# A macaron transformer block on one core: abs ahead of relu in the stick-breaking scores, and ten steps of the mixer in another place

## The chip, the cores and the metric

The kernel runs on one core of one Trainium2 chip. The metric is the device time of one execution in microseconds (us). The engines are named as in the profile: PE is TensorE (matmuls), DVE is VectorE, ACT is ScalarE, POOL is GpSimd, and SP issues the DMAs. Each engine works through its own list of instructions in order; they meet only at semaphores.

## What is computed

One block of three sublayers over 512 tokens of width 1024, in float32, each with RMSNorm and a modulation (`ada`) from a conditioning vector: a SwiGLU FFN of width 2816, a token mixer, and a second such FFN. The mixer, cut to what matters here:

```python
def stick_breaking_attention(q, k, v):          # 8 heads of 64
    z = einsum('bqhd,bkhd->bhqk', q, k) * scale
    log_beta = log_sigmoid(z)
    log_keep = where(strict, log_beta - z, 0.0)
    suffix = cumsum(log_keep, axis=3, reverse=True) - log_keep
    w = where(strict, exp(log_beta + suffix), 0.0)
    return einsum('bhqk,bkhd->bqhd', w, v)

def forgetting_attention(q, k, v, log_f_cum):   # 8 heads of 64, q and k normed
    z = einsum('bqhd,bkhd->bhqk', q, k) * scale + log_f_cum(q) - log_f_cum(k)
    return einsum('bhqk,bkhd->bqhd', softmax(where(causal, z, -inf)), v)

proj = h @ w_in                                  # q, k, v of both kinds, gates, forget logits
mix = concatenate([rmsnorm(o_sb), rmsnorm(o_fx) * sigmoid(fox_gate)]) @ w_out
x = x + gate * mix
```

## The kernel before

**Stages.** The first FFN runs to about 400 us of the trace, the mixer from there to about 730 us, the second FFN after it. Weights are not used as they are: each tile of 128x1024 is split into a rounded high part (`w_hi`, ACT, L1107) and the rest (`w_lo`, DVE, L1471), and each product is three matmuls (L694 to L696). Four raw tiles and two split ones are kept at a time; the load of tile t by SP waits until tile t-4 is split.

**Jobs and units.** The mixer has eight jobs of two heads each: jobs 0 to 3 are stick-breaking, 4 to 7 forgetting. A job has five units, each a 128x512 block of scores made up of the causal blocks of one or two query blocks. `(j, u)` below is unit u of job j. The scores of successive units go to bank 2 and bank 3 in turn.

**The order** is one list, `STEPS`, which `mixer_steps` writes out and which PE, ACT, DVE all walk; each engine issues what the step asks of it and skips the rest. So moving a step moves its instructions on every engine that it uses. The kinds of step are:

- `proj` (PE: half a weight tile against h; q, k and gate chunks use bank 0 or 1, v chunks both), `out` (PE: the output projection)
- `split` (ACT then DVE: the next weight tile)
- `evac` (ACT then DVE: a finished chunk is copied out of its bank into q, k or v as high and low part; for a gate chunk DVE first copies it, L1781, then ACT makes the sigmoid in three passes, L1303 to L1307)
- `scores` (PE, L960 to L962), `prep`, `sum`, `exp` (the pointwise work, below), `turn` (PE: transpose, L984), `unload` (ACT L1402 then DVE L1889: the transposed block as `pt_hi` and `pt_lo`)
- `values` (PE: weights times v into bank 6; half 0 needs units 0 to 2 of its job unloaded, half 1 all five)
- `square`, `stat`, `scale`, `part` (the RMSNorm of a head pair: ACT squares, L1331; PE takes the mean, L1012; ACT makes 1/rms, L1338 and L1340, DVE multiplies, L1804; ACT and DVE write high and low part, for o L1349 and L1816, for q L1356 and L1823)
- `forget`, `decay` (the forget gates' running sum, and its rows on PE, L1021, and ACT, L1366).

**A stick-breaking unit** goes through a chain: scores on PE; in `prep` DVE takes relu of the bank (L1839, `relu_done`), then ACT takes abs of the same bank (L1374), exp (L1376) and ln (L1378); in `sum` DVE scans (L1867) and subtracts (L1871); in `exp` ACT takes exp (L1394); PE turns, ACT and DVE unload. ACT's abs waits for `relu_done`:

```python
act.wait_ge(relu_done, unit + 1)        # ACT, L1371
if unit >= 2:
    act.wait_ge(scan_done, unit - 1)
a(buf, bank[2 + unit % 2][:], ACT.Abs).then_inc(abs_done, 1)
```

Within one unit's period DVE's list reads: relu, scan, subtract, the low part of an `evac`, the low part of a `split`, the low part of the unload of the unit before, and then the relu of the next unit. ACT's reads: abs, exp, ln, high parts of `evac`, `split` and unload, the unit's last exp, and then the abs of the next unit.

Of the kernel before, what the change touches and what calls it, by code (L numbers as in the profile page):

```python
# [22 lines left out]
SBJ = 4  # L23
# [67 lines left out]
def halves_due(p):  # L91

    return int(6 + 1.65 * min(p + 1, 5) + 1.55 * min(max(p - 4, 0), 20) + 0.95 * max(p - 24, 0))


def mixer_steps():
# [13 lines left out]
    steps, norms, chains, evacs, splits = [], [], [], [], []  # L110
# [3 lines left out]
    def emit(*step):  # L114
        steps.append(step)
        spent[0] += array.get(step[0], 0)
# [154 lines left out]
    for n in range(4):  # L271
        emit("out", n, KC - 1, KC)
    assert not queue
    return steps, norms


STEPS, NORMS = mixer_steps()


def hybrid_block_kernel(  # L280
# [4 lines left out]
    with ctx:  # L285
        def sem(name):
            return ctx.enter_context(nc.semaphore(name))
# [14 lines left out]
        def keep(name, shape, dt=F32):  # L302
# [127 lines left out]
        s_done, relu_done, abs_done, eneg_done, e_ready, scan_done, d_ready, p_ready_sb = (  # L430
            sem("s_done"), sem("relu_done"), sem("abs_done"), sem("eneg_done"), sem("e_ready"),
            sem("scan_done"), sem("d_ready"), sem("p_ready_sb"))
# [656 lines left out]
        def _(act):  # L1089
# [176 lines left out]
            for step in STEPS:  # L1266
# [93 lines left out]
                elif kind == "decay":  # L1360
                    _, j, h = step
# [5 lines left out]
                elif kind == "prep" and step[1] < SBJ:  # L1367

                    unit = 5 * step[1] + step[2]
                    buf = tmp_a[:, unit % 2, :]  # L1370
                    act.wait_ge(relu_done, unit + 1)  # L1371
                    if unit >= 2:
                        act.wait_ge(scan_done, unit - 1)
                    a(buf, bank[2 + unit % 2][:], ACT.Abs).then_inc(abs_done, 1)  # L1374
# [4 lines left out]
                elif kind == "prep":  # L1379

                    _, j, u = step
                    unit = 5 * j + u
# [8 lines left out]
                elif kind == "exp" and step[1] < SBJ:  # L1391
                    unit = 5 * step[1] + step[2]
                    act.wait_ge(d_ready, unit + 1)
                    a(tmp_b[:, unit % 2, :], tmp_b[:, unit % 2, :], ACT.Exp).then_inc(p_ready_sb, 1)  # L1394
                elif kind == "unload":
                    _, j, u = step
                    unit = 5 * j + u
# [53 lines left out]
            for tb in range(TB):  # L1451
# [5 lines left out]
                  scale=1.0 / D).then_inc(fln_done, 1)  # L1457
# [5 lines left out]
        def _(dve):  # L1463
# [201 lines left out]
            with dve.Fori(0, UP_BLOCKS) as i:  # L1665
                for q in range(4):
                    f, j = 4 * i + 2 + q, q % 2
# [61 lines left out]
            for step in STEPS:  # L1729
# [101 lines left out]
                elif kind == "prep":  # L1831
                    _, j, u = step
                    unit = 5 * j + u
                    zb, buf = bank[2 + unit % 2], tmp_b[:, unit % 2, :]
                    dve.wait_ge(s_done, unit + 1)
                    if unit >= 2:
                        dve.wait_ge(t_done, unit - 1)
                    if j < SBJ:
# [18 lines left out]
                elif kind == "sum" and step[1] < SBJ:  # L1857

                    _, j, u = step
                    unit = 5 * j + u  # L1860
# [11 lines left out]
                elif kind == "sum":  # L1872
                    _, j, u = step
                    unit = 5 * j + u
# [9 lines left out]
                elif kind == "unload":  # L1884
                    _, j, u = step
                    unit = 5 * j + u
# [79 lines left out]
```

## Time and profile before

| what | us |
|---|---|
| median of 3 runs | 1145.46 |
| lowest, highest | 1144.56, 1147.65 |
| profiled execution, its time | 1145.88 |
| its span in the trace | 1144.1 |

The profiled execution lies 0.42 us above the median, and 1.8 us of it are outside the span. PE is busy for 1108.5 us of the span. The granted clock is TensorE's: 1.00 is 2.4 GHz, 0.50 is 1.2 GHz. In the rows of the trace a matmul's end is modelled and overlaps the start of the next, so that an idle time of PE is some 0.2 us shorter in a row than the time by which the next matmul is late; the prediction says where it adds that.

### The profile page before, as it was taken

How to read it: one execution, taken by the hardware profiler on the slowest of the kernel's cores; microseconds unless marked ns; L12 is line 12 of the kernel's file. 1: busy time of each engine (PE TensorE's matmuls, PEld its weight loads, DVE VectorE, ACT ScalarE, POOL GpSimd, SP SyncE). 2: the span in 40 equal slices, each digit the busy share in tenths (PEclk: the TensorE clock that was granted, in tenths of full speed). 3: DMA queues.
4: the chain of work that ended last, by engine and by line, in shares of the span. 5: the costliest groups of instructions: out<-in, count | busy, mean ns of one | idle time of the engine just before them, and what ended most of it. 6: DMA issues, size and time to landing. Idle time of an engine off the chain costs nothing.

```text
span 1144.1 us, 14298 instructions
## 1 busy us (share of the span) xinstructions
PE 1108.5 (97%) x5142; PEld 885.2 (77%) x5142; DVE 596.1 (52%) x829; ACT 446.4 (39%) x693; POOL 71.7 (6%) x68
## 2 busy tenths in 40 slices
PE   8999999999999999889999999999999999999997
PEld 5788888888788868678778767778888888878876
DVE  3746464655644556777766677663333333434343
ACT  5522222222222235566776665353222222312312
POOL 1000000000000001000000000000000000225350
PEclk9999999999999999999999999999999999999999
DMA  9755675565573631221212211332333333223221
GB/s 343 212 148 165 195 207 166 165 190 165 166 227 105 193 92 47 80 67 44 73 52 66 65 47 42 89 91 74 92 97 96 97 94 92 74 83 98 96 92 74
DMA packets 169687, 133.32 MB, mean 117 GB/s; under 512 B 5436, under 2 KB 150956, under 8 KB 169644
## 3 DMA queue, kind: packets, MB, share of 16 engines
q1 hardware_dynamic: 168704, 130.60, 38.0%
q0 software_dynamic: 768, 2.10, 0.8%
q8 instruction: 26, 0.43, 0.2%
q14 instruction: 17, 0.14, 0.0%
q10 hardware_dynamic: 172, 0.06, 0.0%
HBM read 128.54 MB, written 2.10 MB: 114 GB/s over the span
## 4 chain that ended last, share of the span: by engine, by line
PE 76%; DVE 12%; ACT 7%; issue 3%; DMA 1%; SPq 0%; DVEq 0%; ACTq 0%
PE bank L694 24%; PE bank L696 24%; PE bank L695 24%; DVE w_lo L1471 2%; DVE tmp_b L1867 2%; DVE pt_lo L1889 1%; PE bank L714 1%; ACT w_hi L1107 1%; ACT tmp_a L1376 1%; DVE tmp_b L1839 1%; ACT tmp_a L1374 1%; ACT tmp_a L1378 1%; DMA w_raw<-in_w_ffn_down_dram 1%; PE bank L1012 1%; DVE tmp_b L1871 1%
## 5 line engine op out<-in xcount | busy, mean ns | idle before, releaser
L1471 DVE TENSOR_TENSOR w_lo<-w_raw,w_hi 128x1024 fp32r<-128x1024 f32 x163 | 216.9, 1332 | 382.6 <-ACT w_hi L1107 382.1
L694 PE MATMUL bank<-h_hi,w_hi 128*128 128x512 f32 x864 | 349.2, 404 | 1.3 <-DVE v_lo L1772 0.3
L695 PE MATMUL bank<-h_lo,w_hi 128*128 128x512 f32 x864 | 342.9, 397 | 0.0
L696 PE MATMUL bank<-h_hi,w_lo 128*128 128x512 f32 x864 | 342.8, 397 | 0.0
L1107 ACT ACTIVATE w_hi<-w_raw 128x1024 fp32r<-128x1024 f32 x163 | 172.3, 1058 | 422.2 <-PE bank L696 402.5
L694 PEld LDWEIGHTS bank<-h_hi,w_hi 128*128 128x128 f32 x864 | 163.2, 189 | 44.9 <-issue 5.5
L695 PEld LDWEIGHTS bank<-h_lo,w_hi 128*128 128x128 f32 x864 | 163.1, 189 | 40.6 <-issue 2.6
L696 PEld LDWEIGHTS bank<-h_hi,w_lo 128*128 128x128 f32 x864 | 163.1, 189 | 39.6
L595 POOL TENSOR_TENSOR w_raw<-w_raw,gate_row 128x1024 f32<-128x1024 f32 (+1 forms) x24 | 54.9, 2287 | 378.9 <-DMA w_raw<-in_w_ffn_down_dram 378.6
L694 PE MATMUL bank<-w_hi,hid_hi 128*128 128x512 f32 x176 | 69.9, 397 | 3.2 <-DVE w_lo L1471 3.2
L694 PE MATMUL bank<-hid_hi,w_hi 128*128 128x512 f32 x176 | 70.1, 398 | 1.0 <-DVE w_lo L1471 1.0
L696 PE MATMUL bank<-w_hi,hid_lo 128*128 128x512 f32 x176 | 69.8, 396 | 0.0
L696 PE MATMUL bank<-hid_hi,w_lo 128*128 128x512 f32 x176 | 69.8, 396 | 0.0
L695 PE MATMUL bank<-hid_lo,w_hi 128*128 128x512 f32 x176 | 69.8, 396 | 0.0
L695 PE MATMUL bank<-w_lo,hid_hi 128*128 128x512 f32 x176 | 69.2, 393 | 0.0
L1483 DVE SCALAR_TENSOR_TENSOR ada_acc<-ada_w,cond,ada_acc 128x1024 f32<-128x1024 f32 x49 | 62.7, 1279 | 0.0
L1216 ACT ACTIVATE hid_hi<-tmp_b 128x512 f32 (+1 forms) x44 | 27.8, 632 | 85.6 <-DVE tmp_b L1663 81.1
L1598 DVE TENSOR_TENSOR hid_lo<-tmp_b,hid_hi 128x512 f32 (+1 forms) x44 | 30.5, 692 | 39.7 <-ACT hid_hi L1216 39.6
L1867 DVE TENSOR_TENSOR_SCAN tmp_b<-tmp_a,tmp_b 128x512 f32<-128x512 f32 (+3 forms) x32 | 25.1, 815 | 36.0 <-ACT tmp_a L1378 36.0
L694 PEld LDWEIGHTS bank<-w_hi,hid_hi 128*128 128x128 f32 x176 | 33.0, 188 | 11.7 <-DVE w_lo L1471 4.0
L694 PEld LDWEIGHTS bank<-hid_hi,w_hi 128*128 128x128 f32 x176 | 33.1, 188 | 9.3 <-DVE w_lo L1471 1.4
L696 PEld LDWEIGHTS bank<-hid_hi,w_lo 128*128 128x128 f32 x176 | 33.1, 188 | 8.1
(215 smaller groups left out, 1342.6 us busy)
## 6 DMA issues: line engine op xcount, KB each, us to landing
w_raw<-in_w_ffn_up_dram SPq DMA_DIRECT2D x88, 512.0 KB, 4.6
ada_w<-in_w_ada_dram SPq DMA_DIRECT2D x56, 512.0 KB, 3.6
w_raw<-in_w_ffn_down_dram SPq DMA_DIRECT2D x36, 512.0 KB, 4.4
w_raw<-in_w_in_dram SPq DMA_DIRECT2D x28, 512.0 KB, 3.7
ada_first<-in_w_ada_dram SPq DMA_DIRECT2D x16, 512.0 KB, 10.9
w_raw<-in_w_out_dram SPq DMA_DIRECT2D x8, 512.0 KB, 3.7
w_raw<-in_w_ffn_down_dram SPq DMA_DIRECT2D x8, 384.0 KB, 4.4
x_nat<-in_x_dram SPq DMA_DIRECT2D x4, 512.0 KB, 5.2
```

The lines of the kernel that those rows point to most:

```text
L595: g.tensor_tensor(tile, tile, gate_row[:, :, half * 512:(half + 1) * 512] .broadcast_to([P, nk, 512]), ALU.mult).then_inc(w_gated, 1)
L694: mm(dst, wh, xh, start=start, stop=False, skip_group_check=skip)
L695: mm(dst, wh, xl, start=False, stop=False, skip_group_check=skip)
L696: return mm(dst, wl, xh, start=False, stop=stop, skip_group_check=skip)
L714: last = mm(bank[4 + p][:], cond[:, k:k + 1].broadcast_to([P, P]), ada_first[:, p, k, :], start=k == 0, stop=k == KC - 1)
L1012: mm(bank[7][:], pair_mean[:], ssum[:], start=True, stop=True).then_inc(stat_done, 1)
L1107: a(w_hi[:, s, :], w_raw[:, r, :], ACT.Copy).then_inc(w_hi_done, 1)
L1216: a(hid_hi[:, bass.ds(f, 1), :], tmp_b[:, j:j + 1, :], ACT.Copy).then_inc(hid_hi_done, 1)
L1471: v.tensor_tensor(w_lo[:, s, :], w_raw[:, r, :], w_hi[:, s, :].bitcast(F32), ALU.subtract)\
L1483: ins = v.scalar_tensor_tensor(ada_acc[:], source, cond[:, k:k + 1], ada_acc[:], ALU.mult, ALU.add)
L1598: v.tensor_tensor(hid_lo[:, bass.ds(f, 1), :], tmp_b[:, j:j + 1, :], hid_hi[:, bass.ds(f, 1), :].bitcast(F32), ALU.subtract).then_inc(hid_ ...
L1867: last = v.tensor_tensor_scan(buf[:, back], tmp_a[:, unit % 2, back], buf[:, back], 0.0, ALU.add, ALU.add)
```

## The change

**The order of abs and relu.** In the stick-breaking units ACT's abs now waits for the scores themselves, and DVE's relu waits for ACT's abs. No instruction is added or removed. The forgetting units keep their wait.

**The moved steps.** After the list is written, ten steps are taken out and put in front of another step, in this order:

```diff
+AHEAD = (
+    (("prep", 0, 1), ("forget", 4)),
+    (("evac", 15), ("scores", 4, 1)),
+    (("split", 83), ("exp", 2, 3)),
+    (("split", 93), ("part", 10)),
+    (("split", 95), ("part", 13)),
+    (("part", 11), ("scores", 6, 1)),
+    (("scores", 2, 0), ("proj", 78, 8, 0)),
+    (("scores", 2, 3), ("stat", 1)),
+    (("proj", 88, 17, 0), ("stat", 7)),
+    (("prep", 6, 1), ("scale", 11)),
+)
...
+    for step, mark in AHEAD:
+        steps.remove(step)
+        steps.insert(steps.index(mark), step)
     return steps, norms
...
-                    act.wait_ge(relu_done, unit + 1)
+                    act.wait_ge(s_done, unit + 1)
                     if unit >= 2:
                         act.wait_ge(scan_done, unit - 1)
                     a(buf, bank[2 + unit % 2][:], ACT.Abs).then_inc(abs_done, 1)
...
-                    dve.wait_ge(s_done, unit + 1)
+                    if j < SBJ:
+                        dve.wait_ge(abs_done, unit + 1)
+                    else:
+                        dve.wait_ge(s_done, unit + 1)
```

Five of the ten go to a later place, though the table is called AHEAD: the gate copy `evac 15`, the splits 83, 93 and 95, and `part 11`. The other five go earlier: two `prep`, two `scores`, and one half of `proj 88`. In the changed kernel the lines after the table are numbered 17 higher, those of DVE's loop behind the new wait 20 higher.

DVE around unit (2, 3), before: `split 83` (the row of `w_lo_52`) stands ahead of the unload of (2, 2) (the two rows of `pt_lo_96`), and relu waits for the scores (`s_done`).

```order
L1792 TENSOR_TENSOR k_l_b_94<-bank1,k_hh_b_93 64x512
L1471 TENSOR_TENSOR w_lo_52<-w_raw_50,w_hi_51 128x1024 [waits w_hi_done]
L1889 TENSOR_TENSOR pt_lo_96<-bank4,pt_hi_95 128x2x128 [waits pt_hi_done]
L1889 TENSOR_TENSOR pt_lo_96<-bank4,pt_hi_95 128x2x128
L1839 TENSOR_SCALAR tmp_b_70<-bank2 128x512 [waits t_done,s_done]
```

The same place now:

```order
L1809 TENSOR_TENSOR k_l_b_94<-bank1,k_hh_b_93 64x512
L1909 TENSOR_TENSOR pt_lo_96<-bank4,pt_hi_95 128x2x128 [waits pt_hi_done]
L1909 TENSOR_TENSOR pt_lo_96<-bank4,pt_hi_95 128x2x128
L1488 TENSOR_TENSOR w_lo_52<-w_raw_50,w_hi_51 128x1024 [waits w_hi_done]
L1859 TENSOR_SCALAR tmp_b_70<-bank2 128x512 [waits t_done,abs_done]
```

The unload has passed the split, and relu waits for `abs_done`.

PE ahead of the first v tile of chunk 8, before: the scores of unit (1, 4) into bank 3, then `proj 78`, whose first matmul waits until the chunk before it is out of bank 0 and 1 (`v_ready`).

```order
L960 MATMUL bank3<-k_hh_b_93,q_st_92 128x512 [waits d_ready]
L961 MATMUL bank3<-k_l_b_94,q_st_92 128x512
L962 MATMUL bank3<-mask_strict_55,ident_bf_54 128x128
L694 MATMUL bank0<-w_hi_51,h_hi_74 128x256 [waits v_ready,w_lo_done]
L695 MATMUL bank0<-w_lo_52,h_hi_74 128x256
```

Now:

```order
L977 MATMUL bank3<-k_hh_b_93,q_st_92 128x512 [waits d_ready]
L978 MATMUL bank3<-k_l_b_94,q_st_92 128x512
L979 MATMUL bank3<-mask_strict_55,ident_bf_54 128x128
L977 MATMUL bank2<-k_hh_a_99,q_st_92 128x512 [waits d_ready,qk_ready,k_twice0]
L978 MATMUL bank2<-k_l_a_100,q_st_92 128x512
L979 MATMUL bank2<-mask_strict_55,ident_bf_54 128x128
L711 MATMUL bank0<-w_hi_51,h_hi_74 128x256 [waits v_ready,w_lo_done]
```

The scores of unit (2, 0) have come between the two; the scores of (2, 3) go ahead of `stat 1` and `proj 80` in the same manner.

DVE around job 6's first units, before: `scale 11` (`nrm_104`), `sum` of (6, 0), `part 11` (the low part of q for job 7), the unload of (5, 4), and then `prep` of (6, 1) from bank 3.

```order
L1804 TENSOR_TENSOR nrm_104<-bank0,rstd_73 128x512 [waits nrm_lo,nrstd_done]
L1878 RECIPROCAL small_68<-small_68 128x1 [waits exp_done,nrm_f32]
L1882 TENSOR_SCALAR tmp_b_70<-tmp_b_70,small_68 128x512 [waits inv_done]
L1823 SCALAR_TENSOR_TENSOR q_st_92<-nrm_104,gq8_66,q_st_92 64x512 [waits nrm_hi]
L1823 SCALAR_TENSOR_TENSOR q_st_92<-nrm_104,gq8_66,q_st_92 64x512
L1889 TENSOR_TENSOR pt_lo_96<-bank5,pt_hi_95 128x4x128 [waits pt_hi_done]
L1849 ISA tmp_b_70,small_68<-bank3,f_keys_101 128x384 [waits exp_done,t_done,s_done]
```

Now:

```order
L1869 ISA tmp_b_70,small_68<-bank3,f_keys_101 128x384 [waits exp_done,t_done,s_done]
L1869 ISA small_68 128x1
L1869 ISA tmp_b_70,small_68<-bank3,f_keys_101 128x128
L1869 ISA small_68 128x1
L1875 TENSOR_SCALAR small_68<-small_68 128x2 [waits max_done]
L1821 TENSOR_TENSOR nrm_104<-bank0,rstd_73 128x512 [waits nrm_lo,nrstd_done]
L1898 RECIPROCAL small_68<-small_68 128x1 [waits exp_done,nrm_f32]
L1902 TENSOR_SCALAR tmp_b_70<-tmp_b_70,small_68 128x512 [waits inv_done]
L1909 TENSOR_TENSOR pt_lo_96<-bank5,pt_hi_95 128x4x128 [waits pt_hi_done]
L1840 SCALAR_TENSOR_TENSOR q_st_92<-nrm_104,gq8_66,q_st_92 64x512 [waits nrm_hi]
L1840 SCALAR_TENSOR_TENSOR q_st_92<-nrm_104,gq8_66,q_st_92 64x512
```

`prep` of (6, 1) now leads, and the unload has passed `part 11`.

## Rows read from the trace of the kernel before

**Rows 1.** Busy time, share of the span and instructions of each engine, from the page.

```profile
PE 1108.5 (97%) x5142; PEld 885.2 (77%) x5142; DVE 596.1 (52%) x829; ACT 446.4 (39%) x693; POOL 71.7 (6%) x68
```

**Rows 2.** Windows: stretch, its length, busy us of PE, PEld, DVE, ACT, POOL; clock.

```profile
442.00:600.00 158.00, 143.93 (x804) 118.40 (x803) 111.28 (x165) 108.95 (x187) 5.13 (x11) 0.98 0.24 64
600.00:730.00 130.00, 124.49 (x662) 100.28 (x662) 87.25 (x225) 79.62 (x170) 3.08 (x6) 1.00 0.21 57
```

**Rows 3.** Waits of PE, 442 to 600 us: total us, times, longest.

```profile
PE bank L694 <- DVE pt_lo L1889: 6.6, 3, 2.9
PE bank L1012 <- ACT ssum L1331: 3.0, 3, 2.0
PE bank L694 <- DVE v_lo L1772: 1.5, 2, 1.1
PE bank L984 <- ACT tmp_b L1394: 1.4, 2, 0.8
```

**Rows 4.** Waits of PE, 600 to 730 us.

```profile
PE bank L1012 <- ACT ssum L1331: 2.0, 2, 1.2
PE bank L694 <- DVE pt_lo L1889: 1.4, 1, 1.4
PE bank L1012 <- ACT f_keys L1366: 1.0, 1, 1.0
```

**Rows 5.** Windows at half clock, columns as in Rows 2.

```profile
477.00:480.40 3.40, 3.40 (x16) 3.33 (x15) 1.47 (x2) 3.30 (x6) 0.00 (x0) 0.51 0.41 131
583.00:586.20 3.20, 3.20 (x9) 2.52 (x8) 2.25 (x5) 2.96 (x6) 0.00 (x0) 0.50 0.03 5
```

**Rows 6.** Groups by line, from the page: busy us, mean ns, idle before, releaser.

```profile
L1867 DVE TENSOR_TENSOR_SCAN tmp_b<-tmp_a,tmp_b 128x512 f32<-128x512 f32 (+3 forms) x32 | 25.1, 815 | 36.0 <-ACT tmp_a L1378 36.0
```

**Rows 7.** Waits of ACT, 442 to 600 us.

```profile
ACT tmp_a L1374 <- DVE tmp_b L1839: 27.1, 18, 2.8
```

**Rows 8.** Timeline of DVE, unit (0, 3): start, us, instruction, idle before and releaser.

```profile
466.23 1.23 DVE L1471 TENSOR_TENSOR w_lo<-w_raw,w_hi 128x1024 fp32r<-128x1024 f32 x1
467.48 0.76 DVE L1889 TENSOR_TENSOR pt_lo<-bank,pt_hi 128x384 fp32r<-128x384 f32 x2
468.15 0.68 DVE L1839 TENSOR_SCALAR tmp_b<-bank 128x512 f32<-128x512 f32 x1
470.90 1.27 DVE L1867 TENSOR_TENSOR_SCAN tmp_b<-tmp_a,tmp_b 128x384 f32<-128x384 f32 x2 [2.06 <-ACT tmp_a L1378]
```

**Rows 9.** Timeline of ACT beside it.

```profile
465.41 0.63 ACT L1394 ACTIVATE tmp_b<-tmp_b 128x512 f32<-128x512 f32 x1
468.87 0.60 ACT L1374 ACTIVATE tmp_a<-bank 128x512 f32<-128x512 f32 x1 [2.83 <-DVE tmp_b L1839]
```

**Rows 10.** Timeline of PE: the scores of unit (2, 0), then the next projection.

```profile
518.81 0.48 PE L960 MATMUL bank<-k_hh_a,q_st 128*128 128x512 f32 x1
519.12 0.40 PE L961 MATMUL bank<-k_l_a,q_st 128*128 128x512 f32 x1
...
519.40 0.37 PE L694 MATMUL bank<-w_hi,h_hi 128*128 128x256 f32 x1
```

**Rows 11.** Timeline of ACT: the abs of unit (3, 3), and `square 5`.

```profile
578.66 0.60 ACT L1374 ACTIVATE tmp_a<-bank 128x512 f32<-128x512 f32 x1 [0.83 <-DVE tmp_b L1839]
...
581.11 0.57 ACT L1331 ACTIVATE ssum<-bank 128x512 f32<-128x512 f32 x1
```

**Rows 12.** Timeline of DVE, 547 to 551 us: `split 83`, then the unload of (2, 2).

```profile
548.29 1.23 DVE L1471 TENSOR_TENSOR w_lo<-w_raw,w_hi 128x1024 fp32r<-128x1024 f32 x1
549.54 0.76 DVE L1889 TENSOR_TENSOR pt_lo<-bank,pt_hi 128x256 fp32r<-128x256 f32 x2
```

**Rows 13.** Timeline of DVE, 662 to 667 us: `part 11`, then the unload of (5, 4).

```profile
663.44 1.51 DVE L1823 SCALAR_TENSOR_TENSOR q_st<-nrm,gq,q_st 64x512 fp32r<-64x512 f32 x2 [0.76 <-ACT q_st L1356]
664.98 0.69 DVE L1889 TENSOR_TENSOR pt_lo<-bank,pt_hi 128x512 fp32r<-128x512 f32 x1
```

## The prediction

> **What bounds the kernel now.** I read the windows first. PE is busy for 97% of the span [rows 1]; the mixer is where most of the rest lies. From 442 to 600 us, the stick-breaking jobs, PE idles for 158.0 - 143.9 = 14.1 us, and from 600 to 730, the forgetting jobs, for 130.0 - 124.5 = 5.5 us, while DVE is busy for 111.3 of the first 158 us and ACT for 109.0 [rows 2]. So no engine beside PE is full: what PE waits for is late, not overloaded. The change touches the mixer alone, and its most is what PE loses there.
>
> The waits of PE say what it lacks. In the first stretch 6.6 us are for DVE's unloads, 3.0 for ACT's squares, 1.5 for DVE's v parts, 1.4 for ACT's last exp, and some 1.2 for smaller things [rows 3]. In the second it is 2.0, 1.4 and 1.0 us for the squares, an unload and a decay row [rows 4].
>
> Two things make these waits dearer than the rows say. A matmul's row overlaps the next: one of 0.48 us starts at 518.81 and the next at 519.12, so its end lies 0.17 us inside it [rows 10]. Each wait costs about 0.2 us more than its idle time. The first stretch has 14 waits over 0.2 us, which I put at 2.4 us more; the second has four longer ones, 0.8 us more. Then the clock: for 3.4 and 3.2 us PE is granted half speed with work on hand [rows 5], which loses 1.7 + 1.6 = 3.3 us. Both come right after PE had stood idle, for 2.9 us at the first and 2.0 at the second, the longest waits of their lines [rows 3]. The whole loss in the mixer is 14.1 + 2.4 + 3.3 = 19.8 and 5.5 + 0.8 = 6.3, together 26 us: the ceiling.
>
> **Abs ahead of relu.** The chain behind the waits is DVE's own list. In all 20 stick-breaking units DVE idles before the scan, 36.0 us in total, until ACT's ln is ready [rows 6]. In unit (0, 3) relu starts at 468.15, abs at 468.87 after ACT had idled for 2.83 us, and the scan at 470.90 after DVE had idled for 2.06 [rows 8, 9]. The two engines take turns at waiting: ACT waits 27.1 us for relu, in 18 of 20 units [rows 7].
>
> Now ACT goes ahead by itself. Its exp of the unit before starts at 465.41 and takes 0.63 us, so abs could start at 466.07, 2.8 us earlier; the scores are there by then, since relu was held up by DVE's own list (split, unload, relu follow each other without a gap), not by PE. Abs to scan takes 470.90 - 468.87 = 2.03 us, so ln is ready at 468.1, before DVE is through with split, unload and relu at 468.84. The scan starts then: the 2.06 us are gone. A unit takes 158.0 / 20 = 7.9 us on average now; DVE is busy for 5.6 of it, ACT for 5.4, and PE's own work is (158.0 - 19.8) / 20 = 6.9 [rows 2]. DVE's period can fall by the 1.8 us of waiting per unit to 6.1. Then PE is the slowest of the three, and its waits on these chains should vanish, save those whose chain starts at PE itself.
>
> I walked the three lists by hand with the durations of the trace from (0, 1) to (4, 0), starting each instruction when its own engine and what it waits for are done. That walk is an estimate; what it leaves in the first stretch: the chunk ahead of `proj 76` is out of its bank 0.3 us late. Ahead of `proj 78` PE waits 1.1 us [rows 3] for a chunk that it has itself just finished (ACT then DVE copy it), and this stays but for the move below. And `stat 5`: abs of (3, 3) waits 0.83 us for relu and `square 5` ends at 581.68 [rows 11]. The wait of 0.83 goes, and nothing else, since ACT has come from `stat 4`, which PE released. So of 2.0 + 0.2 us at `stat 5`, 1.4 are left. Everything else of the 16.5 us goes, and the first half-clock stretch with it, since the 2.9 us ahead of it go. The second follows a wait that shrinks from 2.0 to 1.2-1.4 us; the two other waits for unloads, 6.6 - 2.9 = 3.7 us together [rows 3], were followed by full speed, so I take it as gone and keep 1.6 us for the range.
>
> **The moved steps of the stick-breaking jobs.** The scores of (2, 0) take 519.40 - 518.81 = 0.59 us [rows 10]; ahead of `proj 78` they fill that much of its 1.3 us, and need only what is ready by then (the subtract of unit (1, 3) and the doubled k of job 2). 0.7 are left. The scores of (2, 3) do the same between `values` and `stat 1`, where the square and the v part are late by 0.7 us in two waits: none left. `split 83` behind the unload: in my walk the unload that `values` of job 2 needs ends 0.2 us before PE comes for it, and with `split 83` in front it would be 1.23 us later [rows 12]. The move is worth up to 1.1 us, and it secures what is already counted for that `values`. The tile is used two projections later, and SP's load behind it has 4 tiles of lead: cost nothing. `prep` of (0, 1) ahead of `forget` gains at most 0.6 us on DVE where PE doesn't wait: nothing. The gate copy `evac 15` makes DVE wait no more for PE ahead of `scale 6`, which `proj 87` wants: 0.3 + 0.2 us.
>
> Sum of the first stretch: 19.8 lost, less what is left, 0.3 + 0.7 + 1.4 = 2.4, gives 17.4 us.
>
> **The forgetting jobs.** `proj 88`, its first half, ahead of `stat 7` covers the 1.2 us wait for `square 7` [rows 4] with 3 us of matmuls: 1.4 us. `stat 7` then comes 3 us later, and ACT's exp of (4, 2) queued behind it some 0.5 us later at most, which its turn, 4 us on, doesn't feel. `part 11` behind the unload of (5, 4), and `prep` of (6, 1) ahead of both: the unload starts at 664.98 behind a part of 1.51 us and a wait of 0.76 [rows 13], and PE's `values` waits for it 1.4 us [rows 4]. In the new order DVE first does `prep` (about 1.0 us), ACT its exps, then the unload: I get it 1.2 us earlier, and 0.4 of the 1.6 left. If `prep` finds its scores late, DVE's `scale 11` and `sum` of (6, 0) wait behind it and the turn of (6, 0) with them: bound -0.8. `split 93` and `split 95` behind the exps of their unit let the next unload, prep and decay run about 0.3 us earlier each, felt at two `values` of 0.4 and at waits of 1.0 and 0.8 us: 1.0 in all, between 0 and 1.5.
>
> Sum: 1.4 + 1.2 + 1.0 = 3.6 us.
>
> **Total.** 17.4 + 3.6 = 21.0 us off the profiled execution's 1145.9 gives 1124.9; the median was 0.4 lower: **1124.5 us**. The second FFN only starts earlier. By the ceiling of 26 us no less than 1119.5 is possible.
>
> **A rule against the rows.** DVE's relu now waits for an abs that reads the same bank, where both could in principle read at once; in the rows they never overlap, before and after. The Trainium skill (PSUM — Partial Sum Buffer, PSUM bank collisions raise a hardware error) says that two engines must not access one bank at a time, reads included. By that rule the wait must stay, and its price is an abs of 0.60 us wherever ACT isn't ahead; the trace shows no such overlap either way, and the sum doesn't change.
>
> **Rivals.**
> - **The second half-clock stretch stays**, or one comes elsewhere, because a wait of 1.2 us at `stat 5` is left: 1.6 us more, 1126. The Trainium skill (Perfetto Trace Analysis, Matmul Optimizations) says that TensorE scales with utilization and wants its matmuls back to back; the two rows at 0.50-0.51 agree. It is within the range.
> - **ACT becomes the late one.** In job 3 the norms of q and k of job 4 come in, three ACT passes and a `part` more per unit than its mean of 5.4 us, which brings it near PE's 6.9; and now relu, and with it DVE's whole list, stands behind it. If ACT's waits chain, a third of the first stretch's gain is lost: 1145.5 - 21 + 6 = 1130, between 1128 and 1134. For it: ACT's list is the tightest there. Against: it idles before most abs [rows 7].
> - **The swap brings little**: the waits were PE's own chain after all, and only the moved steps gain, 1 + 1 + 3.6: 1140. Against it are the 20 waits of 2 us in a row [rows 6].
> - **Slower.** In the units with a `stat`, seven of the 20, abs stands behind ACT's 1.27 us of 1/rms, and relu is held back by that and 0.60 us, where before it ran beside them. DVE's splits and unloads queue behind relu, so each costs PE up to 1.9 us, 13 us in all; it decides if ACT reaches abs after DVE reaches relu in nearly every unit, so that nothing of the 17 us is gained and 3.5 us more are lost: 1150. In 18 of 20 units ACT was there first [rows 7].
>
> **How the numbers follow.** The forecast, 1121 to 1127.5, with or without the second stretch: 0.78. ACT late: 0.13. Little: 0.04. Same within 0.3% (3.4 us, about what a measurement of this kernel can tell from no change), by a mishap between these: 0.02. Slower: 0.03. The range reaches from 1120 into the second rival, to 1130. Faster: 0.78 + 0.13 + 0.04 = 0.95.
>
> **What would show it.** The scan's idle time falls from 36.0 us to under 8, abs starts without a wait for relu, PE's waits for the unloads nearly vanish in the first stretch, its windows at 0.50 go, and `stat 5` and `proj 78` are the waits left. I am wrong if relu waits long for abs, or if PE's idle time from 442 us on stays over 8 us.

## The result, and the profile after

| kernel | median us | runs, lowest to highest |
|---|---|---|
| before | 1146.49 | 4, 1144.56 to 1147.65 |
| after | 1125.49 | 4, 1124.56 to 1126.07 |

The ratio is 0.9818, with a 95% interval of 0.98 to 0.9835: 21.0 us less, against a forecast of 1124.5 us and a range of 1120 to 1130. The profiled execution of the changed kernel took 1125.46 us with a span of 1123.7 us; that of before, 1145.88 and 1144.1.

**Busy time and windows of the changed kernel.** First the line of the page that answers to [rows 1], then the windows that answer to [rows 2]. The stretches are those between the same steps of the program, to about 1 us; they lie up to 20 us earlier. Columns: stretch, length, busy us of PE, PEld, DVE, ACT, POOL, the granted clock, DMA share, GB/s.

```profile
PE 1101.7 (98%) x5142; PEld 882.4 (79%) x5142; DVE 597.4 (53%) x829; ACT 445.2 (40%) x693; POOL 71.7 (6%) x68
```

```profile
442.00:582.40 140.40, 139.02 (x813) 116.78 (x812) 114.03 (x168) 108.89 (x187) 7.15 (x14) 1.00 0.29 74
582.40:710.00 127.60, 124.38 (x665) 100.46 (x664) 87.19 (x225) 78.52 (x169) 2.06 (x4) 1.00 0.21 58
```

PE idles for 140.4 - 139.0 = 1.4 us in the stick-breaking jobs, where it was 14.1, and for 127.6 - 124.4 = 3.2 us in the forgetting jobs, where it was 5.5. In the first stretch DVE and ACT do the same work in 17.6 us less. No window of this execution in the mixer is at half clock; those of [rows 5] have no counterpart.

**PE's waits of the changed kernel**, 440 to 585 us and then 585 to 712 us (total us, times, longest), against [rows 3] and [rows 4]:

```profile
PE bank L1029 <- ACT ssum L1348: 0.6, 1, 0.6
PE bank L711 <- DVE v_lo L1789: 0.5, 1, 0.5
```

```profile
PE bank L977 <- DMA k_hh_b<-k_hh_b: 1.4, 1, 1.4
PE bank L977 <- DMA k_hh_a<-k_hh_a: 0.8, 1, 0.8
PE bank L711 <- DVE w_lo L1488: 0.5, 1, 0.5
```

Lines have moved by 17 to 20. In the first stretch only `stat 5` and `proj 78` are left. In the second, the waits for the squares, the unload and the decay row are gone, and there are two that before did not have: the scores of jobs 6 and 7 wait for a DMA, the doubled k. (The last row, at 707.81, lies behind the mixer's last step; before has it too.)

**The chain inside a unit.** The scan's group by line, against the 36.0 us of idle time in [rows 6], and DVE's three largest waits for ACT in the stretch from 442 to 583 us:

```profile
L1887 DVE TENSOR_TENSOR_SCAN tmp_b<-tmp_a,tmp_b 128x512 f32<-128x512 f32 (+3 forms) x32 | 25.0, 814 | 5.1 <-ACT tmp_a L1395 3.9
```

```profile
DVE tmp_b L1859 <- ACT tmp_a L1391: 7.6, 10, 2.1
DVE w_lo L1488 <- ACT w_hi L1124: 6.1, 4, 2.3
DVE tmp_b L1887 <- ACT tmp_a L1395: 3.9, 7, 0.7
```

The same unit (0, 3) as in [rows 8, 9], on DVE and then on ACT:

```profile
463.79 0.76 DVE L1909 TENSOR_TENSOR pt_lo<-bank,pt_hi 128x384 fp32r<-128x384 f32 x2
464.47 0.68 DVE L1859 TENSOR_SCALAR tmp_b<-bank 128x512 f32<-128x512 f32 x1
465.18 1.27 DVE L1887 TENSOR_TENSOR_SCAN tmp_b<-tmp_a,tmp_b 128x384 f32<-128x384 f32 x2
```

```profile
461.24 0.64 ACT L1411 ACTIVATE tmp_b<-tmp_b 128x512 f32<-128x512 f32 x1
461.76 0.60 ACT L1391 ACTIVATE tmp_a<-bank 128x512 f32<-128x512 f32 x1
462.39 0.63 ACT L1393 ACTIVATE tmp_a<-tmp_a 128x512 f32<-128x512 f32 x1
463.06 0.63 ACT L1395 ACTIVATE tmp_a<-tmp_a 128x512 f32<-128x512 f32 x1
```

ACT takes abs straight behind the exp of the unit before, exp and ln follow, and ln is done at 463.69, 0.78 us before DVE even begins relu. The scan then starts behind relu without a gap. DVE's relu does wait for abs in 10 of 20 units, 7.6 us in all, and its splits wait 6.1 us for ACT's high part, where it was 3.0 before (442 to 600 us). So some of the waiting has moved to other places of DVE's list; PE does not feel it.

**A ruler for small terms.** Executions come to the mixer at different times, with the same instructions ahead of it: over the profiled executions of this study the scores of unit (0, 0) start between 442.87 and 445.59 us. That is more than most moves are worth. Part of it is the clock: the three latest, 444.96 (without proj 88), 445.38 (without split 93, 95) and 445.59 (without split 83), are the ones with a half-clock stretch of 3.4 us ahead of the mixer, at 46 or at 306 to 307 us. So small terms are read as the time between two instructions of PE, the first matmul of one step to the first of another. The three marks in the changed kernel are the scores of (0, 0), `proj 87` and the last `out` step of the mixer:

```profile
443.96 0.47 PE L977 MATMUL bank<-k_hh_a,q_st 128*128 128x512 f32 x1
...
581.07 0.47 PE L711 MATMUL bank<-h_hi,w_hi 128*128 128x512 f32 x1
...
706.48 0.39 PE L711 MATMUL bank<-o_hi,w_hi 128*128 128x512 f32 x1
```

and in the kernel before:

```profile
442.92 0.47 PE L960 MATMUL bank<-k_hh_a,q_st 128*128 128x512 f32 x1
...
598.57 0.47 PE L694 MATMUL bank<-h_hi,w_hi 128*128 128x512 f32 x1 [0.31 <-DVE nrm L1804]
...
726.81 0.39 PE L694 MATMUL bank<-o_hi,w_hi 128*128 128x512 f32 x1
```

The first way, through the stick-breaking jobs, went from 155.65 to 137.11 us, 18.5 less. The second, through the forgetting jobs, went from 128.24 to 125.41, 2.8 less. From the last mark to the end of the span it is 417.3 and 417.2 us: what the mixer gains is kept to the end. The mixer gained 21.4 us; the span shows 20.4, because this execution came to the first mark 1.04 us later. Another profiled execution of the same kernel, below, came to it at 442.98, and its span was 1123.0.

The two ways for every kernel of the study, worked out like this:

| kernel | way 1 | way 2 |
|---|---|---|
| before | 155.65 | 128.24 |
| after | 137.11 | 125.41 |
| after, again | 137.10 | 125.39 |
| the swap alone | 140.74 | 128.25 |
| the moves alone | 154.21 | 125.39 |
| exp waits for relu | 149.43 | 125.48 |
| without split 93, 95 | 137.14 | 125.50 |
| splits behind the parts | 137.11 | 124.93 |
| two other moves | 137.12 | 125.84 |
| without part 11, prep (6, 1) | 137.11 | 126.60 |
| without proj 88 | 137.12 | 125.17 |
| without the scores | 138.26 | 125.72 |
| without split 83 | 138.33 | 125.37 |
| without prep (0, 1) | 137.92 | 125.47 |

Where an edit touches only one of the ways, the other repeats to 0.04 us in way 1. Way 2 repeats as well where PE has no DMA wait in it (128.24 and 128.25 for before and the swap alone). Where it has, it varies from 125.37 to 125.72 us, by 0.35, between kernels that don't differ there.

### The profile page after: what moved, and what is told of

The parts are those of the page before. It is cut to its first block, busy times and chain, and to the rows that moved or that the text cites. A ratio compares the mean times of both kernels' runs of the same rounds, so it can differ in the third digit from the quotient of the medians.

```text
span 1123.7 us, 14298 instructions
## 1 busy us (share of the span) xinstructions
PE 1101.7 (98%) x5142; PEld 882.4 (79%) x5142; DVE 597.4 (53%) x829; ACT 445.2 (40%) x693; POOL 71.7 (6%) x68
## 4 chain that ended last, share of the span: by engine, by line
PE 89%; DVE 3%; ACT 3%; DMA 3%; issue 1%; SPq 0%; DVEq 0%; POOL 0%; ACTq 0%
PE bank L711 27%; PE bank L713 27%; PE bank L712 27%; PE bank L1029 1%; PE bank L731 1%; PE bank L1001 1%; PE bank L977 1%; DMA w_raw<-in_w_ffn_down_dram 1%; DVE w_lo L1488 1%; ACT w_hi L1124 1%; PE bank L978 1%; DMA x_nat<-in_x_dram 1%; DMA k_hh_b<-k_hh_b 0%; PE bank L1062 0%; PE bank L757 0%
## 5 line engine op out<-in xcount | busy, mean ns | idle before, releaser
L713 PEld LDWEIGHTS bank<-w_hi,hid_lo 128*128 128x128 f32 x176 | 33.0, 188 | 8.5
```

Of the source, the lines that this page charges most:

```text
L713: return mm(dst, wl, xh, start=False, stop=stop, skip_group_check=skip)
```

## The experiments

**1. The swap alone.** None of the ten moves:

```diff
-    for step, mark in AHEAD:
+    for step, mark in ():
```

> The changed kernel with abs ahead of relu, but none of the ten moved steps. Theory (the wait that DVE's scan and ACT's abs took in turns is the loss of the first stretch): of the 17.4 us counted for that stretch the moves bring some 2.3 at most (0.8 at proj 78, 0.7 at stat 1, 0.5 at proj 87, and part of split 83), so the swap alone gives 1146.5 - 15 = 1131 us, the scan's idle time falls from 36.0 us to under 8 and both half-clock windows are gone. Rival (PE waited on chains that it starts itself, and only a new order hides them): the scan's idle time falls all the same, but the time stays at 1140 or more, and the idle time of PE between 442 and 600 us at 10 or more of its 14.1 us.

Measured: 1131.32 us (4 runs, 1130.8 to 1132.45) against 1145.62 for the kernel before on that chip, ratio 0.9881 (0.9866 to 0.9897). The scan's idle time is down to 5.7 us, way 1 to 140.74. The theory holds: the swap alone brings 14.3 of the 21 us, all of it in way 1, and way 2 is untouched (128.25). The moves bring 3.6 us more in way 1, not 2.3. The scan's group of this kernel:

```profile
L1887 DVE TENSOR_TENSOR_SCAN tmp_b<-tmp_a,tmp_b 128x512 f32<-128x512 f32 (+3 forms) x32 | 25.0, 813 | 5.7 <-ACT tmp_a L1395 4.5
```

**2. The moves alone.** ACT's abs waits for relu as before:

```diff
-                    act.wait_ge(s_done, unit + 1)
+                    act.wait_ge(relu_done, unit + 1)
...
-                    if j < SBJ:
-                        dve.wait_ge(abs_done, unit + 1)
-                    else:
-                        dve.wait_ge(s_done, unit + 1)
+                    dve.wait_ge(s_done, unit + 1)
```

> The ten moved steps without the swap: ACT's abs waits for DVE's relu as before. Theory (the swap carries the first stretch): the second stretch gives what it gave in the changed kernel, 2.3 to 3.6 us, the first some 1 to 2.5, so 1141 to 1143 us, with the scan's 36 us of idle time in place and a half-clock stretch left. Rival (the moves carry it): 1133 us or less. If the sum of this gain and that of the swap alone is well under the 21.0 us of both, each needs the other; if it is 21, they are independent.

Measured: 1142.61 us (10 runs, 1140.78 to 1143.32) against 1145.62, ratio 0.9975 (0.9965 to 0.9984). Way 2 gains its whole 2.85 us, as in the changed kernel. The medians differ by 3.0 us, so the first stretch gains next to nothing from the moves without the swap; with it they are worth 3.6. The two gains are not independent: 14.3 + 3.0 = 17.3, and together they make 21.0. In the traces of way 1 it is 14.9 + 1.4 = 16.3 against 18.5, so the gap is 3.7 us by the medians and 2.2 by the traces. PE's largest waits in this kernel, 442 to 600 us:

```profile
PE bank L711 <- DVE pt_lo L1906: 7.6, 3, 3.1
PE bank L1029 <- ACT ssum L1348: 3.3, 4, 2.2
PE bank L1001 <- ACT tmp_b L1411: 2.2, 1, 2.2
PE bank L977 <- DVE tmp_b L1888: 1.1, 1, 1.1
```

A step that PE takes early is of use only if what it needs is there. With DVE late, the scores of (2, 3), moved ahead, wait 1.1 us for DVE's subtract (the last row), a wait that [rows 3] does not have. The unloads cost 7.6 us, where they cost 6.6 before.

**3. Where the gain of the swap comes from.** ACT still goes first with abs, but its exp waits for relu:

```diff
                     act.wait_ge(abs_done, unit + 1)
+                    act.wait_ge(relu_done, unit + 1)
                     a(buf, buf, ACT.Exp, scale=-1.0).then_inc(eneg_done, 1)
```

> The changed kernel, but ACT's exp of a stick-breaking unit also waits for DVE's relu of the same unit: ACT still takes abs first, but its exp and ln no longer run beside DVE's split, unload and relu. Theory (the gain is that exp and ln, 2.03 - 0.60 = 1.4 us a unit, are through before DVE comes to the scan): the scan idles for about 1.4 us in each of the 20 units, 25 to 30 us in total, PE's waits for the unloads come back, and the time is 1136 to 1142 us. Rival (the gain is that relu and abs no longer alternate, that is the order of the first two alone): 1125 to 1130 us.

Measured: 1137.83 us (4 runs, 1136.19 to 1138.38) against 1145.78, ratio 0.9932 (0.9916 to 0.9948). The scan's wait in DVE's list, 442 to 600 us:

```profile
DVE tmp_b L1888 <- ACT tmp_a L1396: 23.4, 18, 1.5
```

In 18 units it is 1.5 us at the longest, the exp and ln that can no longer run beside relu, and 12.3 us of way 1 are lost again (1.7 of them by a half-clock stretch that this execution has at 488 us, behind a wait of 2.1). In total it is a little less than the 25 to 30 us expected; the time is within what the theory gave. Against experiment 6, on the same chip, the kernel is 13.1 us slower: that much hangs on exp and ln being through before DVE comes to the scan.

It is not the whole gain of the swap. This kernel is still 4.8 us faster than the moves alone, by the medians and in way 1 alike (154.21 to 149.43; the two ran on different chips, whose medians of before differ by 0.2 us), and the two differ only in abs going first. So of the 17.8 us between the moves alone and the changed kernel about 13 are exp and ln, and about 5 are abs itself, which no longer waits behind DVE's list. The rival names this smaller part.

**4. Without the moves of split 93 and 95**, which were to bring 1.0 us:

```diff
-    (("split", 93), ("part", 10)),
-    (("split", 95), ("part", 13)),
```

> The changed kernel without two of its moves: split 93 and split 95 stay behind the parts 10 and 13. In the changed kernel the scores of jobs 6 and 7 wait 0.8 and 1.4 us for the doubled k that POOL's DMA writes, which they did not before. Theory (a split ahead of the part holds the part back by its own length, and with it that DMA): both waits are gone, PE idles for about 1 us instead of 3.2 between 582 and 710 us, and the time is 1123.5 us or less. Rival (the moves were worth the 1.0 us that the prediction gave them, and the DMA is late for another reason): the two waits stay, or unloads are late by as much, and the time is 1125.5 to 1126.5 us.

Measured: 1124.49 us (5 runs, 1124.18 to 1127.22) against 1145.62, ratio 0.9823 (0.9809 to 0.9836), which can't be told from the changed kernel; the 1123.5 us or less that the theory expected did not come. In the trace both waits for k are gone, as the theory said; but the waits of 1.0 us for the decay row and 0.8 us for `square 14` of [rows 4] are back, and way 2 is 125.50 us. The rows of 585 to 725 us:

```profile
PE bank L1027 <- ACT f_keys L1381: 1.0, 1, 1.0
PE bank L1027 <- ACT ssum L1346: 0.8, 1, 0.8
```

The moves shift 2 us of waiting from one place to another and are worth 0.1, less than way 2 varies by. The reason that the theory gave is wrong, see the next one.

**5. The same splits right behind the parts:**

```diff
-    (("split", 93), ("part", 10)),
+    (("split", 93), ("exp", 5, 3)),
...
-    (("split", 95), ("part", 13)),
+    (("split", 95), ("exp", 6, 3)),
```

> The changed kernel with split 93 and split 95 right behind the parts 10 and 13, instead of ahead of them. Theory (the part's delay is the whole cost of the two moves): the waits for the doubled k are gone as in the kernel without these moves, and since the splits still stand where they do now to within one step, the time is the same as that kernel's or up to 1 us lower: 1122.5 to 1123.5 us. Rival (it is the place of the splits behind the exps that brings the late k): 1125.5 us, like the changed kernel.

Measured: 1124.77 us (5 runs, 1123.85 to 1125.71) against 1145.62, ratio 0.9822 (0.9809 to 0.9836). No wait for k, the other two waits are there, way 2 is 124.93 us: 0.5 less than in the changed kernel and 0.6 less than in experiment 4, which has no wait for k either. That is by single traces; the medians can't tell it, and the 1122.5 to 1123.5 us expected did not come.

Why k was late shows in the issues. In the changed kernel SP issues the load of a weight tile (SPq) as soon as `split 93` is done with the tile's buffer, and that is within 0.2 us of POOL's two DMAs for k:

```profile
632.90 0.38 SPq L622 DMA_DIRECT2D w_raw<-in_w_out_dram  x1
```

```profile
633.09 0.52 POOL L585 DMA_DIRECT2D k_hh_a<-k_hh_a  x1 [50.95 <-ACT k_hh_a L1375]
633.59 0.52 POOL L587 DMA_DIRECT2D k_hh_a<-k_hh_a  x1
```

The DMA table of 630.5 to 639 us (issues, KB each, median us to landing):

```profile
w_raw<-in_w_out_dram SPq DMA_DIRECT2D x1, 512.0 KB, 5.2
k_hh_a<-k_hh_a POOLq DMA_DIRECT2D x2, 128.0 KB, 4.8
```

and PE, which begins the scores when k is there, 5.0 us behind the second issue:

```profile
638.59 0.50 PE L977 MATMUL bank<-k_hh_a,q_st 128*128 128x512 f32 x1 [0.79 <-DMA k_hh_a<-k_hh_a]
```

In the kernel before, SP's load went out 4.1 us ahead of POOL's, and had landed when POOL's began; its two issues and its DMA table, 648 to 657 us:

```profile
648.42 0.38 SPq L605 DMA_DIRECT2D w_raw<-in_w_out_dram  x1
```

```profile
652.56 0.52 POOL L568 DMA_DIRECT2D k_hh_a<-k_hh_a  x1 [50.02 <-ACT k_hh_a L1358]
```

```profile
w_raw<-in_w_out_dram SPq DMA_DIRECT2D x1, 512.0 KB, 3.8
k_hh_a<-k_hh_a POOLq DMA_DIRECT2D x2, 128.0 KB, 2.7
```

With the splits behind the parts SP's load goes out 2.7 us behind POOL's (634.42 and 631.72), and k lands in 2.9 us, the tile in 3.8. The DMA table of that kernel, 629 to 637.5 us:

```profile
w_raw<-in_w_out_dram SPq DMA_DIRECT2D x1, 512.0 KB, 3.8
k_hh_a<-k_hh_a POOLq DMA_DIRECT2D x2, 128.0 KB, 2.9
```

So the two transfers slow each other, by 2.1 us for k and 1.4 us for the tile. All 14 profiled kernels agree. In nine of them the load goes out 0.2 us ahead of k, for jobs 6 and 7 both; there each of k's DMAs takes 4.5 to 5.7 us to land, the tile 5.0 to 6.1, and PE waits for k. In the other five the load goes out 4.1 us ahead or 2.7 behind; k takes 2.6 to 3.5 us, the tile 3.6 to 3.8, and PE doesn't wait. The Trainium skill (DMA: Bandwidth & Descriptors, Issuing engines are not separate DMA queues) says that DMAs of the scalar, sync and GpSimd engines run on the same DMA engines and interleave; these rows agree. A part held back by the split is not enough to make PE wait: counted from the second mark, POOL issues at 633.09 - 581.07 = 52.0 us in the changed kernel and at 635.01 - 582.52 = 52.5 us without the moves, so k is even issued 0.5 us earlier. The split does hold k back, by 0.95 us against this experiment's kernel, where POOL issues at 631.72 - 580.65 = 51.07; but with 2.9 us to landing k would still be there ahead of PE.

**6. The changed kernel again**, beside the next ones.

> The changed kernel itself, to stand beside the next ones on the same chip. Every theory expects 1125 to 1126 us, and the waits of 0.8 and 1.4 us for the doubled k in the forgetting jobs.

Measured: 1124.78 us (5 runs, 1124.6 to 1126.51) against 1145.78, ratio 0.9821 (0.9806 to 0.9836), ways of 137.10 and 125.39 us.

**7. Two other moves in place of the splits'.** An attempt at a better kernel:

```diff
-    (("split", 93), ("part", 10)),
-    (("split", 95), ("part", 13)),
...
+    (("decay", 6, 1), ("split", 94)),
+    (("scores", 7, 3), ("stat", 14)),
```

> The changed kernel without the moves of split 93 and 95, and with two other moves against the waits that then come back: decay (6, 1) ahead of split 94, so that ACT copies that row 1.05 us earlier, and scores (7, 3) ahead of stat 14, so that PE computes for 1.0 us while ACT squares. Theory (these waits of 1.0 and 0.8 us are one ACT instruction out of place each, and can be had without holding back a part): neither wait is left, PE idles for about 1 us between 582 and 712 us, and the time is 2.3 us under the changed kernel's: 1122.5 to 1123.5 us. Rival (as with split 93 and 95, what is moved makes something else late by as much): 1124.5 us or more, with a new wait in its place.

Measured: 1125.25 us (5 runs, 1125.2 to 1127.27), ratio 0.9825 (0.981 to 0.984), way 2 125.84 us. The rival was right. PE's waits, 600 to 725 us:

```profile
PE bank L1001 <- DVE tmp_b L1902: 0.9, 2, 0.7
PE bank L711 <- DVE w_lo L1488: 0.5, 1, 0.5
PE bank L711 <- DVE pt_lo L1909: 0.4, 1, 0.4
PE bank L1029 <- ACT f_keys L1383: 0.3, 1, 0.3
```

The wait for the square is gone and that for the decay row is down to 0.3 us (the row of `w_lo` lies behind the mixer's last step), but the turn of (6, 0) now waits 0.7 us for DVE and the `values` behind it 0.4. PE came to them earlier, and what they need did not. By the traces this is slower by 0.3 us in way 2 than the kernel of experiment 4, and neither has a DMA wait. PE is 0.7 us earlier at `stat 11`, counted from the second mark, and 0.5 us later at `stat 12`: the wait that was filled in front of a chain of DVE and ACT came back behind it. No kernel of this study is measurably faster than the changed one.

**8. Without part 11 and prep (6, 1) moved:**

```diff
-    (("part", 11), ("scores", 6, 1)),
...
-    (("prep", 6, 1), ("scale", 11)),
```

> The changed kernel without the moves of part 11 and prep (6, 1). Theory (by the prediction these two bring 1.2 us, at the values of job 5): that values step waits 1.4 us for its unload again, where the changed kernel has no wait, and the time is 1.2 to 1.6 us over the changed kernel's: 1126.5 to 1127. Rival (the wait for the doubled k just ahead takes it in): the wait for k at the scores of job 7 shrinks by as much, and the time is the changed kernel's.

Measured: 1126.16 us (4 runs, 1125.55 to 1126.31), ratio 0.9827 (0.9811 to 0.9843), way 2 126.60 us, 1.2 more than the changed kernel. PE's wait for the unload is back at 1.4 us and k's waits are nearly as they were (0.9 and 1.3): the theory holds.

Experiments 9 to 12 have two runs each, on a chip on which the changed kernel itself was not run; the median of before there is 1146.47 us. What they show is read from the ways of one trace each.

**9. Without proj 88 moved:**

```diff
-    (("proj", 88, 17, 0), ("stat", 7)),
```

> The changed kernel without the move of proj 88: stat 7 comes first again. By the prediction the move covers a wait of 1.2 us and brings 1.4: PE's wait for square 7 is back at 1.0 to 1.2 us, and the way from proj 87 to stat 10 is 1.2 to 1.4 us longer than the changed kernel's 46.0 us, so 1126.5 us. Rival (stat 7 in its new place holds up ACT and DVE, and the gain is given back before stat 10): the way is longer by under 0.6 us.

Measured: 1125.88 us (2 runs, 1125.35 and 1126.42), ratio 0.9823 (0.9795 to 0.9852). PE has no wait at all at `stat 7`, and from `proj 87` to `stat 10` it takes 46.25 us against 46.03 in the changed kernel and 47.5 both before and with the swap alone. The rival's number came true (under 0.6 us), for a reason that neither side had: `evac 15` had already taken the wait away. With the swap alone that step stands earlier and DVE waits 2.0 us at it for PE:

```profile
582.24 0.69 DVE L1798 TENSOR_SCALAR sig<-bank 128x512 f32<-128x512 f32 x1 [1.96 <-PE bank L713]
```

Its `scale 6`, `part 6` and `prep` of (4, 1) come as much later, ACT waits for them, and `square 7` ends at 594.07, 10.4 us behind the start of `proj 87`. Without `proj 88` moved it ends at 591.21, 9.1 us behind it. So of the 1.5 us at this place 1.3 go to the gate copy and 0.2 to `proj 88`. (The gate copy's move was not undone by itself. Of the other moves only that of `split 93` reaches between these two steps, and without it the way is the same 46.03 us.) In way 2 as a whole nothing is left of the 0.2: it is 125.17 us here, 0.2 less than in the changed kernel, because the two waits for k are shorter, 0.7 and 0.9 us.

**10. Without the scores (2, 0) and (2, 3) moved:**

```diff
-    (("scores", 2, 0), ("proj", 78, 8, 0)),
-    (("scores", 2, 3), ("stat", 1)),
```

> The changed kernel without the moves of the scores (2, 0) and (2, 3). By the prediction they bring 0.6 us ahead of proj 78 and 0.7 at stat 1: PE waits 1.1 us ahead of proj 78 and 0.3 us ahead of stat 1, and the way from the scores (0, 0) to proj 87 is 1.0 to 1.3 us longer than the changed kernel's 137.1 us, 1126.5 us. Rival (what PE gains there it waits for at the values of job 2): longer by under 0.5 us.

Measured: 1126.06 us (2 runs, 1125.94 and 1126.17), ratio 0.9825 (0.9796 to 0.9853). Way 1 is 138.26 us, 1.16 more. The wait at `proj 78` is 1.1 us and that at `stat 1` 0.35. The theory holds.

**11. Without split 83 moved:**

```diff
-    (("split", 83), ("exp", 2, 3)),
```

> The changed kernel without the move of split 83: it stands ahead of the unload that the values of job 2 wait for. By the prediction up to 1.1 us: the kernel with the swap alone waited 0.9 us at these values, so the wait is back at about 0.9 us, and the way from the scores (0, 0) to proj 87 is 0.9 to 1.1 us longer, 1126 us. Rival (the scores moved ahead of proj 78 have shifted that unload, or prep (0, 1) has): no wait there, and the same time as the changed kernel.

Measured: 1127.64 us (2 runs, 1126.87 and 1128.42), ratio 0.9838 (0.981 to 0.9867). PE waits 0.9 us for the unload at the `values` of job 2, way 1 is 138.33, 1.22 us more, which is the split's own length on DVE [rows 12].

**12. Without prep (0, 1) moved:**

```diff
-    (("prep", 0, 1), ("forget", 4)),
```

> The changed kernel without the move of prep (0, 1): DVE does the forget step first. The prediction gave this move nothing, but the 0.3 us that it expected PE to be late at proj 76 are not there in the changed kernel and are there with the swap alone. Theory (the start of the first units, 0.6 us earlier on DVE, is felt up to proj 76): the wait of 0.3 us at proj 76 is back, the way to proj 87 is 0.3 to 0.6 us longer. Rival (another of the moves took it away, or nothing did): that way is the same to 0.1 us.

Measured: 1126.95 us (2 runs, 1126.39 and 1127.51), ratio 0.9832 (0.9804 to 0.9861). The wait of 0.3 us at `proj 76` is back and way 1 is 137.92, 0.8 us more, where 0.3 to 0.6 were expected: 0.25 us are lost ahead of `stat 0`, the rest at `proj 76`.

## Why the prediction was right, and where it was not

**The total.** 21.0 us were forecast and 21.0 measured between the medians. The mixer gained 21.4 in the traces, 18.5 in way 1 and 2.8 in way 2, against 17.4 and 3.6. PE's idle time from 442 us on is 1.4 + 3.2 = 4.6 us, under the 8 us that were to be the sign of an error. That the totals agree to 0.1 us is luck: 1.1 us too little in the first stretch and 0.8 too much in the second cancel, and the interval of the ratio is 2 us wide to either side. The time itself came out 1.0 us over the forecast of 1124.5, as much as the median of before rose with its fourth run, from 1145.46 to 1146.49. Two small slips of the sum change nothing: [rows 3] and the three smaller waits make 13, not 14, and at 0.2 us each they cost 2.6 us, not 2.4. Point by point:

**Abs ahead of relu.** The step that carried it, that ACT's 2.03 us from abs to scan come out of the chain because ACT can run them beside DVE's split, unload and relu, was right: the scan's idle time went from 36.0 to 5.1 us, and experiment 3 shows that it is this overlap, about 13 us by exp and ln and 5 by abs. DVE's period was limited by turns of waiting, and PE was the slowest of the three once they were gone. The rivals "ACT becomes the late one" and "slower" are out: relu waits 7.6 us for abs, in 10 units, and PE's waits for unloads are nil. "The swap brings little" is out by experiment 1, 14.3 us. No run here lets relu and abs read the bank at once, so whether the wait between them could be dropped was not tried.

**What is left in the first stretch** was put at 0.3 + 0.7 + 1.4 = 2.4 us, and is 0.5 + 0.2 at `proj 78` and 0.6 + 0.2 at `stat 5`, 1.5. `proj 78` was right. `stat 5` was sized too high, and its step failed: "the wait of 0.83 goes, and nothing else, since ACT has come from `stat 4`, which PE released". PE began `stat 4` at 574.90, and ACT its 1/rms 1.67 us later, straight behind the last exp of (3, 2), which the same alternation had made late; in the changed kernel it is 1.11 us, from 560.81. The two rows of ACT, before and then after:

```profile
576.05 0.63 ACT L1394 ACTIVATE tmp_b<-tmp_b 128x512 f32<-128x512 f32 x1
576.57 0.60 ACT L1338 ACTIVATE rstd<-bank 128x512 f32<-128x512 f32 x1
```

```profile
561.40 0.63 ACT L1411 ACTIVATE tmp_b<-tmp_b 128x512 f32<-128x512 f32 x1
561.92 0.60 ACT L1355 ACTIVATE rstd<-bank 128x512 f32<-128x512 f32 x1
```

So 0.6 us more went than the 0.83. `proj 76` has no wait, by the next point.

**Prep (0, 1)** was costed at nothing, "0.6 us on DVE where PE doesn't wait". Experiment 12 gives it 0.8 us. PE didn't wait there in the trace of before, but most of it came back at `proj 76`, 40 us later, once the swap had made PE the slowest: an edit was judged by the waits of before, where the edit beside it had changed them.

**Split 83 and the two scores** were up to 1.1 us, and 0.6 + 0.7; experiments 11 and 10 give 1.22 and 1.16.

**The gate copy and proj 88.** Evac 15 was 0.5 us at `proj 87`, and what is left of way 1's 3.6 us after the other moves is 3.63 - 0.81 - 1.22 - 1.16 = 0.44, if the moves add up. But it also carries 1.3 us at `stat 7`, which the prediction gave to `proj 88`; the place had the right price, 1.5 us against 1.4, and the wrong edit. The step missed is that DVE's wait of 2 us for PE holds up all that stands behind it in DVE's list, up to the next unit's `prep`, on which ACT waits.

**Part 11 and prep (6, 1)**: 1.2 us forecast, 1.2 measured in experiment 8. The wait at the `values` is gone altogether, though 0.4 us was to stay.

**Split 93 and 95**: 1.0 us forecast, between 0 and 1.5; measured 0.1. This is the term that failed, in its overlap: it took the load behind the split to cost nothing. What it counted does happen: the waits of 1.0 and 0.8 us go. What it left out is SP's load that hangs on the split. The prediction looked for this load at split 83 (4 tiles of lead, so nothing) and judged it by when the tile is needed; it should have asked what else is on the DMA engines when it starts. The load now starts beside the transfer of k, which lands 0.8 and 1.4 us too late for PE. So way 2 is 1.5 + 1.2 + 0.1 = 2.8 us, not 3.6.

**The half-clock stretches**, 3.3 us of the 17.4, are gone in both profiled executions of the changed kernel. The prediction took them to follow from the two waits, and that is only a tendency. In the kernel of the moves alone PE waits 3.1 us for an unload, longer than both waits ahead of [rows 5]; its windows, of the whole stretch, of that wait, and of what follows it:

```profile
442.00:600.00 158.00, 142.25 (x811) 116.96 (x810) 113.42 (x168) 109.32 (x187) 6.12 (x13) 1.00 0.25 66
```

```profile
486.80:490.00 3.20, 0.10 (x2) 0.08 (x1) 2.65 (x4) 1.53 (x3) 0.00 (x0) 1.00 0.07 21
490.00:493.20 3.20, 3.14 (x21) 2.83 (x21) 1.14 (x2) 2.63 (x5) 0.00 (x0) 1.00 0.00 0
```

The clock stays at full speed, 2.4 GHz. And in the kernel without split 93 and 95 a wait of 1.9 us in the first FFN, where the kernels don't differ, is followed by 0.55:

```profile
306.00:309.50 3.50, 3.45 (x9) 2.70 (x10) 1.85 (x2) 1.45 (x2) 0.00 (x0) 0.55 0.30 80
```

The changed kernel's own execution waits 2.2 us at the same place, longer, and goes on at 1.00.

Over the executions of the study, the mean granted clock of the kernel before is 0.994 to 0.997 in 25 of 26 that were timed beside the experiments and 0.999 in one; with the moves alone it is 0.993 to 0.995 in 8 of 10, 0.999 in the others. In the 40 executions of the changed kernel and its kin that let ACT run ahead, it is 0.998 or 0.999 in 29 and 0.997 in 11. Worked out from these means, (1 - clock) times the span, the kernel before loses 4.5 us to the lower level on average and the 40 lose 2.0. So where PE's waits in the mixer are shorter the lower level is rarer, by an estimate of 2.5 us; that it is the waits that do it is not shown beyond this. The term's 3.3 us is a sample of one execution, and it is where, for the moves alone, way 1 (1.4 us less) and the medians (next to nothing for this stretch) differ.

## What to carry to other kernels

When two engines take turns at one bank or buffer, look which of them has idle time ahead of it and give it the first turn; the gain is what it can then do beside the other's list, here exp and ln above all (13 us) and abs itself (5 us). Price a move of a step by everything that hangs on it: the DMA issue that its release starts and what else is on the DMA engines at that time, and all that stands in the same engine's list behind a wait that it takes along. Small terms are read between two marks in the trace of the same engine, since the start of the stage alone varied here by 2.7 us, and a wait that is filled in front of a chain of other engines can come back behind it, as in experiment 7.

## What the runs showed of the hardware

- Two DMAs of different issuers, started within 0.2 us of each other, slowed each other: in the changed kernel the two of 128 KB took 4.8 us in place of 2.7 (before) to 2.9 (experiment 5) to land, the one of 512 KB took 5.2 in place of 3.8.
- PE's clock after a wait is not decided by the wait's length alone. In single executions waits of 2.9 and 2.0 us (before), 2.1 (experiment 3) and 1.9 (experiment 4) were followed by 0.50 to 0.55, and waits of 2.9 and 3.1 us (the moves alone) and 2.2 (the changed kernel, at 306 us) by 1.00.
- An `ACT` pass that reads the same bank just ahead of DVE's relu costs PE nothing here: relu waited up to 2.1 us for it, 7.6 us in all, and none of PE's waits leads back to it.
